# Inverses by 32-row products, and a router's second choice and back matrices in another place

## What is computed

```python
    _, gi = lax.top_k(gl, 1)
    g_oh = jax.nn.one_hot(gi[..., 0], N_GROUPS, dtype=jnp.float32)
    ...
    top_v, top_i = lax.top_k(el_sel, TOPK_IN_GROUP)
    top_w = jax.nn.softmax(top_v, axis=-1) * g_w[..., None]
    ...
        out = out + jnp.einsum("blef,ble,efd->bld", hid, comb[:, :, g], w_down[g])
```

```python
        sa = jnp.einsum('bhvk,bhk->bhv', S, -kk_t)
        S = (S * w_t[:, :, None, :]
             + sa[..., None] * (kk_t * a_t)[:, :, None, :]
             + v_t[..., None] * k_t[:, :, None, :])
        o_t = jnp.einsum('bhvk,bhk->bhv', S, r_t)
```

## Time and profile before

| | us |
|---|---|
| median of 3 runs | 1339.37 |
| lowest and highest | 1337.52, 1339.75 |
| profiled execution | 1336.89 |
| its span (first to last instruction) | 1335.0 |
| TensorE busy in the span | 1285.1 (96%) |
| VectorE busy | 838.8 (63%) |
| ScalarE busy | 729.1 (55%) |
| heads, eight steps | from 917.8 to 1084.0 |
| router and the experts' start | from 308 to 351 |

### The profile page before, as it was taken

How to read it: one execution, slowest core, us unless ns; L and a number is a source line. 1 busy time by engine, 2 the same in 40 slices (tenths; PEclk the granted TensorE clock), 3 DMA queues, 4 the chain that set the end, 5 groups by cost and what they waited for, 6 DMA issues and landing times.

```text
span 1335.0 us, 22458 instructions
## 1 busy us (share of the span) xinstructions
PE 1285.1 (96%) x7929; PEld 1038.8 (78%) x7929; DVE 838.8 (63%) x1575; ACT 729.1 (55%) x1273; POOL 568.4 (43%) x252
## 2 busy tenths in 40 slices
PE   7999999897999999999999999899999999999997
PEld 6978878786887887877667877576888887788886
DVE  1576466547788888898567888855777763221213
ACT  5574566546666776767583233673433424654544
POOL 5886674350000000000479466554100017788884
PEclk9999999998899999999999998899999999999999
DMA  6654454167799999997477477432100006455552
GB/s 219 195 186 142 128 168 131 64 191 248 226 365 318 320 324 344 318 314 269 133 215 207 118 197 204 152 110 96 50 2 2 18 17 205 158 188 189 179 194 86
DMA packets 128515, 240.07 MB, mean 180 GB/s; under 512 B 16428, under 2 KB 23470, under 8 KB 128420
## 3 DMA queue, kind: packets, MB, share of 16 engines
q1 hardware_dynamic: 116656, 227.12, 51.8%
q10 hardware_dynamic: 11765, 11.67, 3.5%
HBM read 234.57 MB, written 1.05 MB: 176 GB/s over the span
## 4 chain that ended last, share of the span: by engine, by line
issue 43%; PE 26%; POOL 19%; DVE 8%; DMA 2%; ACT 1%; ACTq 0%; POOLq 0%; DVEq 0%
POOL wlo L306 19%; PE bank L330 3%; PE bank L326 3%; PE bank L327 3%; DVE bank L2430 3%; DMA work<-proj 2%; PE bank L2689 2%; PE bank L2703 2%; PE bank L2708 1%; PE bank L2665 1%; PE bank L2753 1%; DVE proj L2349 1%; PE bank L2733 1%; DVE proj L2363 1%; PE bank L2725 1%
## 5 line engine op out<-in xcount | busy, mean ns | idle before, releaser
L306 POOL TENSOR_TENSOR wlo<-raw,whi 128x1024 fp32r<-128x1024 f32 (+1 forms) x232 | 557.4, 2422 | 610.2 <-ACT whi L301 605.7
L301 ACT ACTIVATE whi<-raw 128x1024 fp32r<-128x1024 f32 (+1 forms) x300 | 311.7, 1054 | 254.6 <-PE bank L330 130.1
L326 PE MATMUL bank<-whi,t0h 128*128 128x512 f32 (+1 forms) x552 | 226.4, 410 | 5.4 <-ACT whi L301 2.9
L327 PE MATMUL bank<-whi,t0l 128*128 128x512 f32 (+1 forms) x552 | 220.8, 400 | 0.0
L330 PE MATMUL bank<-wlo,t0h 128*128 128x512 f32 (+1 forms) x552 | 152.6, 399 | 2.6 <-POOL wlo L306 2.5
L326 PEld LDWEIGHTS bank<-whi,t0h 128*128 128x128 f32 x552 | 106.2, 192 | 35.8 <-issue 7.2
L330 PEld LDWEIGHTS bank<-wlo,t0h 128*128 128x128 f32 x552 | 106.1, 193 | 28.4 <-POOL wlo L306 4.6
L327 PEld LDWEIGHTS bank<-whi,t0l 128*128 128x128 f32 x552 | 106.4, 193 | 23.4 <-issue 1.2
L306 DVE TENSOR_TENSOR wlo<-work,whi 128x1024 fp32r<-128x1024 f32 x96 | 113.0, 1219 | 7.6 <-ACT whi L301 7.6
L1660 PE MATMUL bank<-whi,t0h 128*128 128x512 f32 x256 | 106.7, 417 | 0.0
L1661 PE MATMUL bank<-whi,t0l 128*128 128x512 f32 x256 | 102.0, 398 | 0.0
(11 more groups left out here) (528 smaller groups left out, 2462.4 us busy)
## 6 DMA issues: line engine op xcount, KB each, us to landing
raw<-in_w_in SPq DMA_DIRECT2D x96, 512.0 KB, 3.7
raw<-in_w_ff SPq DMA_DIRECT2D x64, 512.0 KB, 3.3
work<-in_w_exp_down SPq DMA_DIRECT2D x68, 256.0 KB, 6.0
work<-in_w_exp_gate SPq DMA_DIRECT2D x62, 256.0 KB, 5.6
work<-in_w_exp_up SPq DMA_DIRECT2D x62, 256.0 KB, 6.9
raw<-in_w_exp_down SPq DMA_DIRECT2D x60, 256.0 KB, 5.7
raw<-in_w_in SPq DMA_DIRECT2D x20, 464.0 KB, 4.0
raw<-in_w_exp_gate SPq DMA_DIRECT2D x34, 256.0 KB, 5.8
```

What stands on the lines that cost most here:

```text
L301: nc.scalar.activation(whi[:, s, 0:width], raw_of(n)[:, 0:width], ACT.Copy).then_inc(hi_ready, 1)
L306: ins = (nc.vector if split_by_vector(n) else nc.gpsimd).tensor_tensor(wlo[:, s, 0:width], raw_of(n)[:, 0:width], whi[:, s, 0:width].bitca ...
L326: nc.tensor.matmul(dst[t][:, 0:width], hi[:, k, r], wh[:, kk, :], start=k == 0 and not begun, stop=False)
L327: nc.tensor.matmul(dst[t][:, 0:width], lo[:, k, r], wh[:, kk, :], start=False, stop=False)
```

## The change

Three things. First, levels 1 to 4 of the inverse work on the four 32x32 blocks of the diagonal (`BLOCK`) in place of the two 64x64 blocks: twice as many products of half the size in each direction; masks and copies take 32 columns instead of 64. At level 4 ScalarE writes the result into the 64-column tiles for levels 5 and 6 by four copies per half, with a 0/1 scale for even and odd blocks. Second, level 0 has no product: `begin_inverse` writes the transposed start in four 32-row products, and `turn_first` turns it on VectorE. With that, in a step: `state` stands behind `below` of level 1; `make_ar` is split into `sum_bonus`, `make_r` and `make_a`, which stand in other gaps; the mean's scaling is folded into the subtraction; and the squares stand behind the mask of level 5. Third, in the router: the second choice and its weights stand before and within the gather, `pe_back` stands in expert 0's block behind its first quarter, with the transposes in other banks, and the copies of `back` and the flag stand behind expert 1 (`dve_back`).

```diff
 def act_router
+            act.wait_ge(e2_arg, 1)
+            nc.scalar.activation(r1[4], r1[4], ACT.Exp).then_inc(e2_done, 1)
             act_gather_half(act, 0)
             act_gather_half(act, 1)
-            act.wait_ge(e2_arg, 1)
-            nc.scalar.activation(r1[4], r1[4], ACT.Exp).then_inc(e2_done, 1)
...
-        BACK_AT = [(1, 0), (1, 256), (3, 0), (3, 256), (6, 0)]
+        BACK_AT = [(3, 0), (3, 256), (6, 0), (6, 256), (7, 0)]
...
 def dve_router
+            order.step(nc.vector.scalar_tensor_tensor(out=el, in0=one1, scalar=-3e38, in1=el, op0=ALU.mult, op1=ALU.add))
+            first_max(one2, el, r1[2], tmp8, "rev8", EG)
+            nc.vector.tensor_tensor(r1[4], r1[2], r1[1], ALU.subtract).then_inc(e2_arg, 1)
...
             for b in range(2):
                 s = slice(4 * b, 4 * b + 4)
                 dve_gather(dve, 0, (b,))
+                if b == 1:
+                    weights()
...
+            split_low(dve, Q_MOE + 3)
             picks((1, 2, 3, 4))
-            split_low(dve, Q_MOE + 3)
...
+            split_low(dve, Q_MOE + 4)
+            split_low(dve, Q_MOE + 5)
+            dve.wait_ge(combed, 1)
...
 def pe_experts, block
                     if not (isinstance(E, int) and E == N_EXP - 1):
                         gate_up(m + q, q, E + 1, 1 - b, (J + last) % 2, i, per)
-                    if q == 1:
+                    if back and q == 0:
+                        pe_back(pe)
+                    if q == (2 if back else 1):
...
-            pe_back(pe)
             pe.wait_ge(xg_low, 1)
...
-            pe.wait_ge(back_ready, 1)
...
 def dve_experts
                 block(J, 1, 1, n + 6)
+                if J == 0:
+                    dve_back(dve, order)
...
 def below
+                        if lev < SMALL:
+                            for r in BLOCK:
+                                mm = nc.tensor.matmul(bank[g][r, v * 32:v * 32 + 32], gram[b][r, u, r], Xs[r, u, :],
+                                                      start=True, stop=True)
+                            continue
...
 def grow
+                    if lev < SMALL:
+                        for v in range(2):
+                            u = 2 * g + v
+                            for r in BLOCK:
+                                nc.tensor.matmul(bank[2 + g][r, v * 32:v * 32 + 32], XDs[b][r, u, :], Ys[r, u, :],
+                                                 start=True, stop=True)
...
 def step on TensorE
-                below(p, b, 0, (0,))
                 if tail:
                     solve(p - 1, c, 0)
...
-                below(p, b, 0, (1,))
-                if tail:
-                    state(p - 1, c)
-                else:
                     conv_part(5, 3)
                 below(p, b, 1)
                 if tail:
+                    state(p - 1, c)
                     outputs(p - 1, c, 0, 0)
...
 def grown on ScalarE
+                    elif lev < SMALL:
+                        nc.scalar.activation(Xm[:, r, 0:32], new[:, 0], ACT.Copy, scale=con("even_blocks"))
+                        nc.scalar.activation(Xm[:, r, 32:64], new[:, 0], ACT.Copy, scale=con("odd_blocks")
+                                             ).then_inc(xm_copied.sem, 1)
+                        nc.scalar.activation(XD[b][:, r, 0:32], new[:, 1], ACT.Copy, scale=con("even_blocks"))
+                        nc.scalar.activation(XD[b][:, r, 32:64], new[:, 1], ACT.Copy, scale=con("odd_blocks")
+                                             ).then_inc(xt_copied, 1)
...
 def begin_inverse
-                    for r in HALF:
-                        nc.vector.tensor_tensor(XD[c][r, g, :], gram[c][r, g, r],
-                                                con("level0_t")[r].unsqueeze(1).to_broadcast([64, 2, 64]),
-                                                ALU.mult).then_inc(inverse_begun, 1)
+                    for r in BLOCK:
+                        order.mark(nc.vector.tensor_tensor(XDs[c][r, g, :], gram[c][r, g, r],
+                                                           con("level0_turned")[r].unsqueeze(1).to_broadcast([32, 2, 32]),
+                                                           ALU.mult))
+
+            def turn_first(p, b):
+
+                order.settle()
+                wait_from(dve, x_made, 2 * (LEV - 1) * p)
+                for g in range(2):
+                    nc.vector.transpose(out=Xs[:, 2 * g:2 * g + 2, :], in_=XDs[b][:, 2 * g:2 * g + 2, :]
+                                        ).then_inc(y_masked.sem, 1)
```

More of the change, by code:

```diff
@@ L1689, in down, with block @@
                 mm.then_inc(quarter_done, 1)
-            def block(J, E, b, m, i=0, per=0, first=False, last=False, added=0):
+            def block(J, E, b, m, i=0, per=0, first=False, last=False, added=0, back=False):
                 for q in range(4):
@@ L1713, in pe_experts @@
                 gate_up(Q_MOE + q, q, 0, 0, 0, 0, 0)
-            pe.wait_ge(back_ready, 1)
             for J in range(NG):
                 n = first_of(J)
-                block(J, EG * J, 0, n, first=True)
+                block(J, EG * J, 0, n, first=True, back=J == 0)
                 if J:
@@ L2578, in build @@
         HALF = [slice(64 * a, 64 * a + 64) for a in range(2)]
+        BLOCK = [slice(32 * q, 32 * q + 32) for q in range(4)]
+        SMALL = 5
+        Xs, Ys = Ym[:, :, 0:32], Xm[:, :, 0:32]
+        XDs = [XD[c][:, :, 0:32] for c in range(2)]
         Wn, Uo = carve(9984, NT, P), carve(10240, NT, P)
@@ L2688, in below @@
                         for r in HALF:
-                            mm = nc.tensor.matmul(o[r], gram[b][r, u, r], ident[r, r] if lev == 0 else Xm[r, u, :],
-                                                  start=True, stop=True)
+                            mm = nc.tensor.matmul(o[r], gram[b][r, u, r], Xm[r, u, :], start=True, stop=True)
                     mm.then_inc(y_made, 1)
@@ L2698, in grow @@
                         pe.wait_ge(xt_copied, XT_COPIES * p + 2 * lev + g - 3)
-                    if lev < LEV - 1:
+                    if lev < SMALL:
[4 more added lines that the diff above has]
+                                                 start=True, stop=True)
+                        for v in range(2):
+                            u = 2 * g + v
+                            for r in BLOCK:
+                                mm = nc.tensor.matmul(bank[2 + g][r, 64 + v * 32:64 + v * 32 + 32], Ys[r, u, :],
+                                                      XDs[b][r, u, :], start=True, stop=True)
+                    elif lev < LEV - 1:
                         for v in range(2):
@@ L3136, in centre, with squares @@
                 order.step(nc.vector.tensor_reduce(mean, by_head(o), AX.X, ALU.add))
-                order.step(nc.vector.tensor_scalar(hmean, hmean, 1.0 / DH, None, ALU.mult))
-                nc.vector.tensor_tensor(by_head(cut(0, p)), by_head(o), per_head(mean), ALU.subtract
-                                        ).then_inc(pair_done.sem, 1)
+                nc.vector.scalar_tensor_tensor(out=by_head(cut(0, p)), in0=per_head(mean), scalar=-1.0 / DH,
+                                               in1=by_head(o), op0=ALU.mult, op1=ALU.add).then_inc(pair_done.sem, 1)
+            def squares(p):
                 dve.wait_ge(*pair_done.at(p + 1))
@@ L3147, in step @@
                 c = 1 - b
-                mask(p, 0)
+                turn_first(p, b)
                 if prep:
@@ L3176, in step @@
                 if not prep:
+                    squares(p - 1)
                     variance(1)
                 mask(p, 5)
+                if prep and tail:
+                    squares(p - 1)
                 if prep:
@@ L3237, in first @@
                 key_and_bonus(0, 0)
-                make_ar(0)
+                sum_bonus(0)
+                make_r(0)
+                make_a(0)
                 make_bk(0, 0)
@@ L3266, in dve_heads @@
             centre(PAIRS - 1)
+            squares(PAIRS - 1)
             variance(2)
```

105 lines of the change are left out of this document (63 added, 42 removed).

## The result

| | before | after |
|---|---|---|
| median, us | 1338.44 (4 runs) | 1351.64 (4 runs) |
| lowest and highest | 1335.96, 1339.75 | 1339.66, 1354.86 |
| mean granted clock of the runs | 0.981 in the profiled one | 0.946 to 0.964 |

The change makes the kernel slower: ratio 1.0099, 95% interval 1.0066 to 1.0131. The profiled execution of after is the fastest of its four (1339.66, clock 0.964). So the trace shows the loss at its smallest; the three others had clocks of 0.946 to 0.954 and took 1349 to 1355.

The account below looks back on a forecast made before the run. TensorE's list of work was taken to bound the heads, and its waiting and low clock the router's end. Heads -16.4 and router -6.0 made -22.4 us: 1336.89 becomes 1314.5, plus 2.5 for the median, 1317; range 1311 to 1335.

Parts of the forecast that it names:

- x = 32: Levels one to four: four 32x32 products side by side repeat every 32 ns, where a pair of 64x64 took 58.
- The clock, put at 1.00 without a term,: Forecast expected clock 1.0 from 325 us on and gave no term to a change of clock in the heads.
- What counts in the levels is therefore how long TensorE needs for a product: Heads' levels: filler stands between products and TensorE never sits idle, so product time sets the levels' time.
- -18.3: Levels one to four: narrower products save 0.57 us a level, over 4 levels and 8 steps, 18.3 us.
- It still covers, barely: Heads' levels: TensorE's 2.5 us per level still covers VectorE's work of at most 2.3 us.
- The edge, -2.0: Edge of a step: VectorE's chain from the grams' masks to below falls from 6.52 to 6.24 us, seven times.
- Step zero, -4.6 with its levels: First step of the heads: below starts at 919.4 instead of 921.72, -2.3 us, besides the levels' saving.
- State, +4.5: State update, 0.64 us, moves behind below of level one, where TensorE is the bound: 0.64 x 7.
- The late copy, +1.7: ScalarE: four copies per half at level four delay the copy of B and K, so grams come 0.25 late, seven times.
- The router, -6.0: Router and experts: expert one's block starts 7.3 us earlier, less 1.3 for a late gate for expert two.
- (b): Rival: half the levels' gain, x = 45 by issue rate, or VectorE takes over; 1325; 0.24 including no router gain.
- (c): Rival: 32-row products run only two at a time, x = 116, a loss, 1375; 0.06 including any other loss.

Follow-up runs that it names:

- half_columns: The wide_products kernel with the products of levels one to four moving only 32 of their 64 columns; ratio 1.0236 to before.
- wide_products: After with 64-row products at all levels again, level zero still on VectorE and state still behind below of level one; ratio 0.9971 to before.
- router_alone: Before with only the router's part of the change (second choice, weights, back matrices moved); ratio 0.9979 to before.
- after_filled: After plus four unread 128x128 filler products on TensorE in the edge's idle time of steps one to six; ratio 1.0037 to before.

## Why the prediction was wrong

The measured time lies above the whole range of 1311 to 1335, and the heads, forecast 16.4 us shorter, are 8.4 longer in the fastest execution. Two steps of the prediction failed, one in what holds at the full clock, the other in the clock itself.

- **x = 32** was right: 0.31 us for the 16 records, 2.47 us a level where 2.5 was forecast. The work fell as forecast: TensorE's busy time in a step went from about 20.2 to 17.4.
- **The clock, put at 1.00 without a term,** is the step that makes the change a loss. Every product in the heads' sum is priced at the clock of the earlier trace rows. It fell in two of the seven steps of the trace (24.7 and 25.1 against 20.2: 9.4 us), and more in the other executions, with clocks of 0.946 to 0.954 and 9 to 15 us more. half_columns against wide_products shows that moving fewer columns in the same time is enough to bring it down; that this is what happens in after is inferred from it, and what the new waiting adds is not settled.
- **"What counts in the levels is therefore how long TensorE needs for a product"** is the step that takes the gain away: -18.3 was passed on whole to the time. The forecast's steps at the full clock were 18.7, the measured ones 20.0 to 20.3, against 20.35 before. Had the clock held, seven such steps would have gained about 1 us (an estimate from 7 x 0.15). What came instead: late issue 0.8 us a step, the copies 0.4 more than forecast, level six 0.3, the edge 0.2. The issue was named only against x, not as a stall of its own. "It still covers, barely" was true of VectorE's masks: no level waits for one.
- **The edge, -2.0**: 0.96 instead of 0.8 for four products, 0.37 instead of 0.44 for the turns; from the start of the grams' masks (980.55) to `below` (987.14) 6.59 us, which is 0.07 longer than before's 6.52, so the term was about zero.
- **Step zero, -4.6 with its levels**: it became 1.8 longer (29.2 against 27.35), with 8 us of half clock instead of 3.4. The edge term was nearly right: `below` of level one starts 4.98 us behind the decays instead of 6.78, 1.8 earlier for a forecast 2.3. But TensorE waits 2.39 us for VectorE ahead of `grow` of level six, which it did not before.
- **State, +4.5**: not measured with 32-row products at the full clock alone. With wide ones, putting it back gave 0.25 us a step, not 0.64, since it waits for the copy of U there. So there the move cost less than forecast.
- **The late copy, +1.7**: too small. Eight copies at 0.20 us instead of 0.11 put the grams 0.4 late, and `below` of level five 0.2.
- **The router, -6.0**: right in its place and in its parts (7.2 for 7.3, one wait of 1.58 for a forecast 1 to 2, 1.8 given back for 1.3), though the wait was for a low half and not for the gate. In the ratio of router_alone 2.8 of it were seen.
- **Rivals.** (b) named VectorE or issue as limits and (c) a loss by x. Late issue did come, as (b) named it, but as a stall beside the products and not as their pitch. The loss came by neither: the price of a product was right, and the clock under all the others changed. A loss by something unnamed had a part of 0.06, and the range left it out.

## What to carry to other kernels

Before narrowing products to save TensorE's time, treat the granted clock as a term: if TensorE holds clock 1.00 while it moves full products without a gap, a variant that moves half as much in the same or less time may lose the clock for all the work around it. Test it cheaply by halving the moved columns and leaving all else alone, or by a filler in the new gaps, before the real rewrite. When a busy engine's work is cut, list what stands just below it (the edge's chain, the copies, the feed of instructions), since that is where the time goes next.

## What the runs showed of the hardware

- Halving the moved columns of 64x64 products, with 19.1 of 20 us busy and as many instructions, took the clock of whole executions from 0.976 to 0.987 (wide_products) down to 0.932 to 0.952 (half_columns), half clock in the traced heads from 27 to 106 us, and cost 2.6%. The records lasted as long with 32 columns as with 64: 8 of them 0.40 us.
- Late issue: with some 518 product records in a step of 20 us TensorE stood still for 0.8 to 1.7 us a step with nothing but "issue" as the reason; with 326 to 340 never. In the stretch shown of after_filled it resumed 2.4 to 2.7 us after a 16 KB instruction fetch began.
- Four 32x32 fp32 products side by side repeat about every 32 ns for each of their two records: 16 records take 0.31 us, where 8 of 64x64 side by side in twos take 0.40.
- ScalarE's copies with a per-partition scale come every 0.20 us where its plain copies of the same size come every 0.11.
- What half clock costs: with 17 to 19 us of it a narrow step, with 2.6 to 2.9 us idle at the full clock, took 25 instead of 20.2 (after); with 23.9 us of it a wide one, with 0.9 idle, 30.3 instead of 19.9 (half_columns).
